# Where the sample's attention pieces stand among the products of the feed-forward stage

## What is computed

```python
h = rms_norm(x, norm1_g) * (1 + scale1) + shift1
q, k, v, u, vg = split(h @ w_in)
o_sb = stick_breaking(q, k_all, v_all, ...)      # k_all, v_all: the cache's pages and the new keys
o_mlp = chunk_spatial_gate(gelu(u), vn, w_s, b_s)
x = x + gate1 * (concatenate([o_sb, o_mlp]) @ w_out)
h2 = rms_norm(x, norm2_g) * (1 + scale2) + shift2
up = h2 @ w_up                                   # 1024 -> 2 x 2816
conv = conv_b + sum(conv_w[i] * shifted(up, i))  # causal, width 3
g_ff, v_ff = split(conv)
x = x + gate2 * ((silu(g_ff) * v_ff) @ w_down)
```

## Time and profile before

| | |
|---|---|
| median of 3 runs | 3535.37 us (3531.87 to 3537.59) |
| profiled execution, time | 3530.1 us |
| profiled execution, span of its instructions | 3528.4 us |
| PE busy | 3294.7 us (93%) |
| DVE, ACT, POOL busy | 1684.9, 1080.3, 1494.9 us (48%, 31%, 42%) |
| chain that ended last, PE's part | 54%, of it the products of `finish_layer` (L1392) 46% |
| page loads | 512 of keys and 512 of values, 256 KB each |
| weight loads of `finish_layer` | 136 of 1024 KB, 16 of 768 KB |

### The profile page before, as it was taken

The page is one execution under the profiler, slowest core; times in us unless marked ns, Lnnn a source line. Parts: engine busy times, 40 slices in busy tenths (PEclk is TensorE's granted clock), DMA queues, the critical chain, the costliest instruction groups (busy, mean ns, idle before and its releaser), DMA issues.

```text
span 3528.4 us, 52997 instructions
## 1 busy us (share of the span) xinstructions
PE 3294.7 (93%) x17710; PEld 2288.5 (65%) x17711; DVE 1684.9 (48%) x2542; ACT 1080.3 (31%) x2337; POOL 1494.9 (42%) x1222
## 2 busy tenths in 40 slices
PE   4799999989999959999998999998999999899999
PEld 1344444436656637777776777776777778777777
DVE  0211212138878825554543553544555354566565
ACT  0221222238889812322210331220232121132220
POOL 0010110126656625554533654543555454565553
PEclk8899999989999979999999999999999999999999
DMA  8411101020110056777777667778677674322222
GB/s 327 164 33 59 54 30 49 30 82 2 49 50 14 2 186 213 247 236 242 254 250 274 210 228 245 235 243 267 220 237 241 225 242 154 103 79 77 72 84 78
DMA packets 237935, 536.85 MB, mean 152 GB/s; under 512 B 26831, under 2 KB 60351, under 8 KB 217705
## 3 DMA queue, kind: packets, MB, share of 16 engines
q1 hardware_dynamic: 207081, 361.36, 31.2%
q10 hardware_dynamic: 30592, 172.24, 13.9%
HBM read 498.96 MB, written 34.55 MB: 151 GB/s over the span
## 4 chain that ended last, share of the span: by engine, by line
PE 54%; DVE 6%; issue 2%; DMA 1%; ACT 1%; SPq 0%; DVEq 0%; ACTq 0%
PE ff_pB L1392 46%; PE s_pZ L962 3%; PE s_pO L976 3%; DVE ff_conv L1672 1%; DVE s_left L1038 1%; DMA ff_act_in<-scratch_catT 1%; DVE ff_x L1599 0%; DVE ff_act_in L1688 0%; PE s_pZ L968 0%; DVE s_stop L1042 0%; ACT ff_conv L1470 0%; DVE ff_conv L1674 0%; DVE ff_rs L1681 0%; DMA s_kpage<-in_cache_k 0%; DVE s_kpage L1665 0%
## 5 line engine op out<-in xcount | busy, mean ns | idle before, releaser
L1392 PE MATMUL ff_pB<-ff_act_in,ff_w 128*128 128x256 f32 (+1 forms) x2496 | 616.3, 391 | 38.4 <-DMA ff_act_in<-scratch_catT 18.4
L1392 PEld LDWEIGHTS ff_pB<-ff_act_in,ff_w 128*128 128x128 f32 x2496 | 474.2, 193 | 150.6 <-issue 64.7
L1727 POOL TENSOR_TENSOR ff_sums<-ff_w 128x512 f32<-128x512 f32 (+1 forms) x152 | 191.4, 1259 | 755.1 <-PE ff_pB L1392 609.6
L417 PE MATMUL in_pA<-in_w,in_hT 128*128 128x512 f32 (+1 forms) x1024 | 449.2, 594 | 1.0 <-DVE in_hT L536 1.0
L1672 DVE SCALAR_TENSOR_TENSOR ff_conv<-ff_raw,k_vecT,ff_conv 128x512 f32<-128x512 f32 x352 | 381.7, 1085 | 84.4 <-ACT ff_raw L1477 78.2
L1392 PE MATMUL ff_pB<-ff_diff_up,ff_sums 128*128 128x256 f32 (+1 forms) x1600 | 391.0, 387 | 26.7 <-DVE ff_x L1599 22.7
L1599 DVE SCALAR_TENSOR_TENSOR ff_x<-ff_pB,k_mod,ff_x 128x256 f32<-128x256 f32 (+2 forms) x448 | 213.9, 480 | 385.2 <-PE ff_pB L1392 382.1
L856 POOL TENSOR_TENSOR at_stop<-at_stop,at_left 128x512 f32<-128x512 f32 (+3 forms) x320 | 311.5, 999 | 181.4 <-ACT at_stop L796 176.0
L1500 ACT ACTIVATE ff_raw<-ff_pB 128x256 f32<-128x256 f32 (+1 forms) x352 | 136.0, 388 | 778.9 <-PE ff_pB L1392 772.9
L1392 PEld LDWEIGHTS ff_pB<-ff_diff_up,ff_sums 128*128 128x128 f32 x1600 | 301.8, 191 | 92.1 <-DVE ff_x L1599 23.5
L1648 DVE TENSOR_TENSOR ff_raw<-ff_raw,ff_pB 128x256 f32<-128x256 f32 (+1 forms) x264 | 111.4, 424 | 483.4 <-PE ff_pB L1392 483.3
(11 more groups left out here) (187 smaller groups left out, 4711.2 us busy)
## 6 DMA issues: line engine op xcount, KB each, us to landing
ff_w<-in_w_units ACTq DMA_DIRECT2D x136, 1024.0 KB, 6.0
s_kpage<-in_cache_k SPq DMA_DIRECT2D x512, 256.0 KB, 3.9
s_vpage<-in_cache_v SPq DMA_DIRECT2D x512, 256.0 KB, 3.1
wada<-in_w_ada SPq DMA_DIRECT2D x8, 3072.0 KB, 11.5
ff_w<-in_w_units ACTq DMA_DIRECT2D x16, 768.0 KB, 5.3
in_w<-in_w_in SPq DMA_DIRECT2D x5, 2048.0 KB, 19.4
in_x<-in_x_prompt SPq DMA_DIRECT2D x16, 512.0 KB, 5.3
ff_act_in<-scratch_catT SPq DMA_DIRECT2D x4, 2048.0 KB, 14.5
```

The costliest lines, as they stand in the source:

```text
L417: last = pe.matmul(pA[0:R, m % 2, :], hT[:, kt, t * R:(t + 1) * R], w[:, kt, col:col + DSB], start=kt == 0, stop=kt == KT - 1)
L1392: last = pe.matmul(into, left[:, kt * P:(kt + 1) * P], right[:, kt, :], start=kt == 0 and p in (1, 2, 5), stop=kt == depth(j) - 1, skip_gr ...
L1727: pool.tensor_tensor(S3, A11, A21, ALU.subtract).then_inc(sums_ready, 1)
```

## The change

Only the cost of a product in `chunk_plan` changes: 1.0 for each product of an up-unit, 0.0 for the products of out- and down-units. With no cost behind them, no piece is placed there.

```diff
@@ -1185,7 +1185,7 @@
             follow[AT_UNIT[DOWN, q, 2], p] = ("diff", (OUT, 0), i)
     for j, p in PRODUCTS:
-        events.append((("mul", j, p), 1.75 * depth(j) / HALVES))
+        events.append((("mul", j, p), 1.0 if UNIT[j][0] == UP else 0.0))
         if (j, p) in follow:
             events.append((follow[j, p], 0.0))
```

## The result

The changed kernel takes 3573.19 us (median of four runs, 3569.22 to 3579.53) against 3533.68 us for the kernel before (four runs too, one more than above): ratio 1.0109, 95% interval 1.0094 to 1.0125. It is 39.5 us slower. The forecast was 17 us slower and a range up to 3585, so the sign and the range held, and the size forecast was less than half of what came.

What follows compares the result with a forecast made beforehand. PE was taken as the bound. Gains of 27, 3 and 10 us against losses of 23, 24, 3, 4, 3 and 1, less 1, gave +17: 3535.4 + 17 = 3552 us, range 3520 to 3585.

Steps and rivals of the forecast that it cites:

- (a): Ends of chunks 0 and 1: waits of 12.2 and 10.5 us and the half clock behind them go; gain 27 us.
- (b): Start: SCORE of step 0 moves 50 us later and its 4.90 us page wait goes; gain 3 us, between 2 and 5.
- (c): Out- and down-units: 18 us of waits leave, 0.4 us for each of 21 units comes back; gain 10 us.
- (d): Page loads in runs of up-units: SP's 17.8 us round is slower than PE; losses 23, 5 and 3 us, chunks 0 to 2.
- (e): DVE's part of a step: WEIGH closer ahead of MOVE delays PE; 4 us in chunk 0, 19 in 1, 3 in 2.
- the sign that I had named: Units 5 to 14 of chunk 0: SP's waits for SUM at nearly 0 would show the forecast right.
- crowding: Page transfers slow each other, all landings taking 6.9 us, not 3.7; 41 us more, 3593; chance 0.12.
- The first rival: Page transfers: crowding makes the time 3593 us, decided by DMA engines staying over some 0.9 busy; chance 0.12.

Runs made afterwards that it cites:

- the closed one: Kernel before with the pieces of every chunk spread over the products below unit 32; 3512.6 us against 3535.0, ratio 0.9941.
- WEIGH early: Changed kernel with each WEIGH placed directly behind its SCORE, other pieces where they stood; 3543.9 us, 1.0029 of the kernel before.
- WEIGH early and pages in time: Changed kernel with constant page numbers and each WEIGH directly behind its SCORE; 3483.7 us, 0.9858 of the kernel before.
- the long run: Not a kernel: stretch of chunk 0 from the end of SUM of step 0 to the start of SCORE of step 11; 195.4 us in the changed kernel.
- half the bytes with slower issues: Changed kernel, each page load from step 1 on fetching 64 of 128 partitions, for timing only; 3617.5 us, 1.0226 of the kernel before.
- constant page numbers: Changed kernel, SP taking page numbers from constants instead of reading the table, for timing only; 3529.6 us, 0.9985 of the kernel before.
- the four kernels: Changed kernel (3573.2 us), and it with constant page numbers (3529.6), with WEIGH directly behind SCORE (3543.9), and with both edits (3483.7).
- The one with down-units alone: Kernel before with the cost of products in down-units alone set to 0, out-units keeping theirs; 3527.7 us, ratio 0.9978.
- the closed one with WEIGH early: Kernel before with pieces spread below unit 32 in every chunk and each WEIGH directly behind its SCORE; 3485.2 us, ratio 0.9853.

## Why the prediction was right and wrong

**(a), the ends of the chunks: right.** Both waits went, no half clock followed them, and one experiment with this part alone gave 22 us. **(b), the start: not refuted, hardly shown.** The wait of 4.9 us went. Keeping pieces away from unit 0 took 3485.2 to 3480.3, 5 us, but the intervals of the two ratios overlap, and keeping them out of all out-units showed no gain (3536.3 to 3536.6).

**(c), out- and down-units: too dear.** I put 0.4 us on each down-unit that has nothing of the sample's in it. With WEIGH early and pages in time, all of chunks 0 to 2 had 15.8 - 14.2 = 1.6 us of waits for x, under 0.1 for each of 21 units. So a down-unit costs next to nothing for being free of pieces. In the changed kernel there are 7.5 us of them all the same (3.9 in chunk 0, none in chunk 1, 3.6 in chunk 2), at down-units behind a WEIGH that stands late in unit 14, 16, 26 or 28. The term of 8 us was met there by luck: its cause was another.

**(d), the pages: right as a mechanism, near in size.** SP's round by itself is 18.1 us in the long run, where I had 17.8 from the earlier trace rows, and the keys of step 11 landed 13.8 us after their first issue, not 12.1 (landings there took 4.4 us at the median, not 3.7): 186.0 us for the chain of 181. In chunk 1 the same chain gave 164.3 against 163. That issue and not bandwidth binds was argued from the earlier trace rows and is now shown from both sides: fewer instructions for the same bytes freed 44 us, half the bytes with slower issues cost 44. The rule that the time of issue is small beside the DMA did not hold here (the Trainium skill, DMA: Bandwidth & Descriptors, "Issuing engines are not separate DMA queues"); eight pages took 8.0 us to issue with the table read and 3.65 without.

**The step that failed is how (d) and (e) add up in chunk 0.** I wrote that SP's pace covers the waits at steps 2, 5 and 8, "which the page waits of the same steps cover", and gave 2 us for a late MOVE that holds SUM, and so SP. The runs show that most of it is paid. The page waits alone cost the long run 22.5 us, the MOVE waits alone 13.6, both together 31.9: of the second, 9.4 are paid on top. A wait at MOVE delays SUM; SP may ask for the next values only after SUM, so it stood for 9.5 us in a queue that was already too slow, and its round went from 18.1 to 19.1 us. I had named this path and priced it at 2, and the sign that I had named, waits of SP for SUM at nearly 0, did not come.

The two stretches side by side (WEIGH early, 1367.0 to 1553.0, against 1371.8 to 1567.2 after) show both what was right in it and what was not. The page waits did shrink, from 21.7 us (0.2 for values) to 14.6, while the waits at MOVE and ahead of SUM rose from 2.4 to 12.3: 7 of 10 us were covered. But PE's busy time for the same matmuls rose from 161.9 to 168.4 us, with a granted clock of 1.00 and 0.97. Those slow matmuls stand behind the waits and delay SUM with them: ahead of SUMs 2, 6 and 8 by 1.4, 2.7 and 1.7 us, where SP stood for 1.6, 1.1 and 3.4. By these lengths some 4 of SP's 9.5 us come from slow matmuls (an estimate: 1.4, 1.1 and 1.7) and the rest from the waits as such; no run separates the two.

The size of (e) in the long run was low as well, 8 for 13.6. With constant page numbers the stretch has 13.0 us of such waits, and 2.4 with WEIGH early besides: they stand at MOVE 2, 5, 6, 7 and 8 and ahead of SUM 1 and 10, and I had counted steps 2, 5 and 8. Another 3.0 are busy time. In all the long run was to take 164 + 17 + 2 = 183 us and took 195.4; from SUM 14 to SCORE 19 it was 77.1 us for 74.3 predicted. These 15 us are about what chunk 0 is longer by than forecast, 22.5 for 8.

**Chunk 1** went nearly as written. Of the 15 steps that I had listed 14 have the wait, 1.29 us each at the weight load of MOVE; step 24, whose WEIGH stands at (4,4), has none, and step 23, which I had not listed, has 2.7. PE itself stands idle for 0.89 us at each: 14.8 us in total, for 19 predicted. Page waits are 7.0 us for 5; with (c) at nothing the chunk is 3.8 us longer where I had 7.5. The events of step 28 repeat to 0.01 us:

```profile
2064.50 0.75 DVE L1038 TENSOR_TENSOR_SCAN s_left<-s_go,s_left 128x256 f32<-128x256 f32 x1
...
2065.24 1.26 POOL L1739 TENSOR_TENSOR ff_raw<-ff_raw,ff_conv 128x512 f32<-128x512 f32 x1 [6.98 <-ACT ff_raw L1483]
2065.29 1.50 DVE L1042 TENSOR_TENSOR s_stop<-s_stop,s_left 128x256 f32<-128x256 f32 x1
```

```profile
2066.84 0.44 PE L968 MATMUL s_pZ<-k_ident,s_stop 128*128 128x128 f32 x2 [0.89 <-DVE s_stop L1042]
```

**Chunk 2** was to lose 2 us net and lost 11.8. Its step of 18.7 us clears SP's round by 0.6, and I took 3 us for uneven landings. It has 6.4 of page waits and 2.8 at MOVE; from SUM 46 to SCORE 54 the four kernels show 130.6 with neither, 134.1 with page waits, 134.0 with MOVE waits and 139.6 with both. Here the two cost more together than apart, 9.0 for 3.5 and 3.4. A margin of 0.6 us would do that, as each fits nearly alone and the sum doesn't; that is argued from these four, not shown by a run with another margin.

I had written that chunk 2 longer by 10 us would mean crowding. It does not: key pages landed in 3.5 us at the median there, 3.9 before, and with constant page numbers, where they took 5.5, no page wait was left. The first rival is out for the long run too: the DMA engines were at 0.84, landings took 4.2 us at the median.

**The clock behind new waits is a term that I left out.** In chunk 0 all of PE's named waits other than that for the chunk's input went from 27.5 to 43.4 us, 15.9 more, while the chunk became 22.5 us longer. The other 6.6 are in the busy column: 567.85 us by the first fence for the same matmuls that took 561.34. Slow matmuls after waits, as at 1468.80, are what makes it up where the timeline shows them. Chunk 1 gives 4.6 us of waits and -0.7 of busy time for +3.8, chunk 2 9.3 and 2.6 for +11.8. I had counted half clock where a wait ends, and not where the change makes new ones. MOVE of step 2 is one:

```profile
1402.77 0.69 PE L968 MATMUL s_pZ<-k_ident,s_stop 128*128 128x128 f32 x2 [2.62 <-DVE s_stop L1042]
1403.25 3.33 PE L1392 MATMUL ff_pB<-ff_act_in,ff_w 128*128 128x256 f32 x8
```

Not every wait has it: with constant page numbers the same wait of 2.62 us, and that of 3.60 at MOVE 8, were followed by full speed. How much of the 6.6 us comes with every execution is open, as PE's busy time in chunk 3, whose order is the same, differs by 4.6 us between these two executions.

## What to carry to other kernels

Before work is packed closer, compute the round of every queue that feeds it, issue time included, and not only the busy share of the DMA engines: here the queue had 6.6 us of slack in a step of 24 and the change took 7.9. Do not let one wait cover another without checking what the first one holds back; where a loop goes engine, buffer, queue, engine, a delay in one part can show up in all of it. Where a step's parts are placed by a planner, the distance between them matters as much as their number: putting a small DVE piece directly behind the SCORE that feeds it was worth 29 us in the changed kernel and 27 (3512.6 to 3485.2) in the closed one.

## What the runs showed of the hardware

The same instruction order took different times with the clock. Chunk 3 is the same in all kernels, and in the stretches from its first matmul to the end it was 519.1 us in the kernel before and 524.7 in the changed one (first fence). The one with down-units alone and the closed one with WEIGH early have:

```profile
3005.20:3525.90 520.70, 488.92 (x2084) 397.20 (x2084) 309.19 (x615) 113.44 (x268) 278.76 (x209) 0.99 0.23 79
```

```profile
2959.70:3485.40 525.70, 494.21 (x2086) 400.85 (x2085) 310.34 (x617) 113.40 (x268) 278.95 (x209) 0.98 0.23 79
```

It is 519 to 521 us where the granted clock is 0.99 and 525 to 526 where it is 0.98, with PE busy 487.4 to 488.9 us in the one case and 492.0 to 494.2 in the other; PE's named waits in this stretch add up to 27.1 to 28.6 us in the four, and the shortest sum stands in one of the long stretches. So of the 46.7 us between the two profiled executions some 5.6 lie in a stretch that the change does not touch, and go with the clock. Why the clock differed is open. I had not expected two executions of one order to differ by 1% in a stretch.

A DMA issue with the page number read from a table took SP 1.0 us (8.04 for eight), 0.46 without, and the shape of the destination changed the instruction itself: 0.34 us for 128 partitions, 0.48 for 64.
